# The running sum's row of a stick-breaking attention: two copies on two engines, or one on VectorE

## The reference, cut to what matters

```
z = q . k / 8                                   # scores of keys against queries
log_1m_beta = where(key < query, log_sigmoid(-z), 0)
between = reverse_cumsum(log_1m_beta) - log_1m_beta     # sum over the keys between
weights = where(key < query, exp(log_sigmoid(z) + between), 0)
out = weights @ v
```

## Time and profile before

| what | us |
|---|---|
| median of 3 runs | 1442.71 |
| lowest, highest | 1438.63, 1443.05 |
| the profiled execution | 1436.79 |
| its span, first to last instruction | 1435.1 |
| TensorE busy (modelled) | 1358.9 |
| VectorE busy | 871.1 |
| ScalarE busy | 676.8 |
| GpSimd busy | 324.5 |

### The profile page before, as it was taken

The page is one execution under the profiler, slowest core; times in us unless marked ns, Lnnn a source line. Parts: engine busy times, 40 slices in busy tenths (PEclk is TensorE's granted clock), DMA queues, the critical chain, the costliest instruction groups (busy, mean ns, idle before and its releaser), DMA issues. The chain is left out here.

```text
span 1435.1 us, 27696 instructions
## 1 busy us (share of the span) xinstructions
PE 1358.9 (95%) x11020; PEld 1063.8 (74%) x11020; DVE 871.1 (61%) x1347; ACT 676.8 (47%) x1249; POOL 324.5 (23%) x434
## 2 busy tenths in 40 slices
PE   6999989999999899898999889999999999999997
PEld 5877767777777566555677678888887788888886
DVE  6244261575752465667365787776665656669865
ACT  5533241352423387878354645445443434345541
POOL 6675544542432042435101300000000000000000
PEclk9999999999999799999999999999999999999999
DMA  6555333533225330404242254445444865787952
GB/s 204 145 156 150 103 82 89 149 85 84 62 75 125 122 75 3 90 2 137 89 156 103 81 165 159 142 147 158 157 136 147 279 194 179 257 269 252 305 188 103
DMA packets 191546, 201.07 MB, mean 140 GB/s; under 512 B 36669, under 2 KB 127994, under 8 KB 191418
## 3 DMA queue, kind: packets, MB, share of 16 engines
q1 hardware_dynamic: 145132, 169.47, 37.5%
q10 hardware_dynamic: 46286, 29.84, 7.5%
HBM read 145.06 MB, written 54.20 MB: 139 GB/s over the span
## 5 line engine op out<-in xcount | busy, mean ns | idle before, releaser
L484 POOL TENSOR_TENSOR fr_wL<-fr_raw,fr_wH 128x256 fp32r<-128x256 f32 (+1 forms) x208 | 164.2, 821 | 76.6 <-PE fr_ps_F L1267 54.2
L1267 PE MATMUL fr_ps_F<-fr_hL,fr_wH 128*128 128x512 f32 (+1 forms) x416 | 167.9, 404 | 2.8 <-DVE fr_hL L804 2.4
L1267 PE MATMUL fr_ps_F<-fr_hH,fr_wH 128*128 128x512 f32 (+1 forms) x416 | 166.6, 400 | 0.0
L1267 PE MATMUL fr_ps_F<-fr_hH,fr_wL 128*128 128x512 f32 (+1 forms) x416 | 113.4, 402 | 0.0
L1267 PEld LDWEIGHTS fr_ps_F<-fr_hL,fr_wH 128*128 128x128 f32 (+1 forms) x416 | 76.6, 184 | 22.9 <-issue 3.1
L2618 PE MATMUL all_ps_b<-ro_hH,ro_slot 128*128 128x512 f32 x272 | 88.4, 391 | 3.0 <-ACT pl_p L2120 1.5
L1267 PEld LDWEIGHTS fr_ps_F<-fr_hH,fr_wL 128*128 128x128 f32 (+1 forms) x416 | 76.2, 187 | 20.0 <-issue 3.2
L1267 PEld LDWEIGHTS fr_ps_F<-fr_hH,fr_wH 128*128 128x128 f32 (+1 forms) x416 | 76.8, 185 | 18.8 <-issue 2.3
L478 POOL CAST fr_wH<-fr_raw 128x1024 fp32r<-128x1024 f32 (+1 forms) x42 | 48.5, 1155 | 160.3 <-PE fr_ps_F L1267 140.0
L2627 PE MATMUL all_ps_b<-ro_hH 128*128 128x512 f32 x312 | 75.9, 389 | 0.0
L2627 PE MATMUL all_ps_b<-ro_y 128*128 128x512 f32 x300 | 72.7, 389 | 0.5 <-DVE ro_y L2454 0.5
(11 more groups left out here) (480 smaller groups left out, 3154.9 us busy)
## 6 DMA issues: line engine op xcount, KB each, us to landing
pl_slot<-in_w_ff SPq DMA_DIRECT2D x88, 256.0 KB, 4.4
pl_slot<-second_operands SPq DMA_DIRECT2D x75, 256.0 KB, 3.7
fr_raw<-in_w_in ACTq DMA_DIRECT2D x37, 512.0 KB, 4.2
second_operands<-pl_hL SPq DMA_DIRECT2D x64, 256.0 KB, 2.0
pl_hT<-in_w_ff SPq DMA_DIRECT2D x44, 256.0 KB, 4.5
projected<-fr_stage ACTq DMA_DIRECT2D x39, 256.0 KB, 4.4
pl_hT<-second_operands SPq DMA_DIRECT2D x37, 256.0 KB, 3.8
pl_xt<-in_w_ff SPq DMA_DIRECT2D x16, 512.0 KB, 5.6
```

Source lines behind the costliest of these rows:

```text
L484: m = pool.tensor_tensor(wL[b][:, k:k + 2, 0:wd], raw[b][:, k:k + 2, 0:wd], wH[b][:, k:k + 2, 0:wd].bitcast(F32), ALU.subtract)
L1267: m = pe.matmul(F[b][0:wd, :], w[b][:, k, 0:wd], a[:, k, :], start=(at_ == 0), stop=(at_ == len(passes) - 1))
```

## The change

The running sum's row is copied once, by VectorE, straight from the bank into row 0 of `SP[(u+2) % 4]`; ScalarE's copy, GpSimd's copy and the four `row` tiles are gone. VectorE makes it for unit u at the head of its turn u+3, before that turn's softplus, and for unit 25 (u = 27, NU - AHEAD) right behind the last softplus. The copy waits for unit u's weight. TensorE's wait before it reuses a bank is now on `placed`, with the same count.

```diff
-        row = [r.sb(f"row{n}", [1, HALF]) for n in range(4)]
@@ gpsimd
                     if not first:
-                        known = UNITS[u - 2][3]
-                        pool.wait_ge(s("handed"), handed(i, u - 2))
-                        pool.wait_ge(s("sp"), i * NU + u + 1)
-                        pool.tensor_copy(SP[u % 4][0:1, known:HALF], row[(u - 2) % 4][0:1, known:HALF]
-                                         ).then_inc(s("placed"), 1)
                         gla(i * NG + NTH[u] - 1)
@@ scalar
-                def hand_on(u):
-                    off = UNITS[u][3]
-                    if u >= 4 and hands_on(u - 4):
-                        act.wait_ge(s("placed"), placed(i, u - 2))
-                    act.copy(row[u % 4][0:1, off:HALF], Z[u % NZ][0:1, off:HALF]).then_inc(s("handed"), 1)
                 for u in range(NU):
                     weight(u)
-                    if hands_on(u):
-                        hand_on(u)
                     if u + AHEAD < NU:
@@ vector
+                def hand_on(u):
+                    off = UNITS[u][3]
+                    dve.wait_ge(s("weight"), i * NU + u + 1)
+                    dve.wait_ge(s("sp"), i * NU + u + 3)
+                    dve.tensor_copy(SP[(u + 2) % 4][0:1, off:HALF], Z[u % NZ][0:1, off:HALF]).then_inc(s("placed"), 1)
+
                 for u in range(NU):
+                    if u >= AHEAD and hands_on(u - AHEAD):
+                        hand_on(u - AHEAD)
                     softplus(u)
+                    if u == NU - 1:
+                        hand_on(NU - AHEAD)
@@ tensor, scores
                     if u >= NZ and hands_on(u - NZ):
-                        pe.wait_ge(s("handed"), handed(i, u - NZ))
+                        pe.wait_ge(s("placed"), handed(i, u - NZ))
```

## The result

The changed kernel takes 1503.66 us (median of 6 runs, 1496.99 to 1508.54). The kernel before, run on the same chip, takes 1441.42 us (6 runs, 1438.63 to 1443.43). The ratio is 1.0432, with a 95% interval from 1.0403 to 1.0460: 62 us slower, where 9 were predicted. The sign was right, the size was not, and the time lies far outside the range.

The account below looks back on a forecast made before the run. No engine plainly full in the heads stage: ScalarE paces part, an engine ring the rest. Order loses 15 us, ScalarE's relief wins 6: 9 us slower, 1451.7 us; range 1440 to 1463, the forecast's own 1447 to 1460.

Parts of the forecast that it names:

- What bounds it: Stage of the heads, 490 to 691 us: no engine plainly full; ScalarE sets the pace in part, an engine ring elsewhere.
- an ordered ring of engines: Over two turns: scores, exponential, logarithm, ratio part, other VectorE work, copy, next scores; 3.4 us plus other work when wide.
- ScalarE's relief, 6 us: 72 row copies leave ScalarE: 1 us won in late pass 2, 5 in narrow stretches; bounds 0 and 20.
- Load on VectorE: 72 copies from PSUM added, about 33 us or 27 by start spacing; VectorE, busy 128 of 201 us, still fits.
- The order term: Heads stage: the copy stands behind VectorE's other work, and TensorE's sums and scores wait; 15 us lost, bounds 2 and 25.
- I take 4 for about five such places: Narrow stretches: short copies, but a few turns have 2 to 4 us of other VectorE work; 4 us lost.
- the 5 us set by analogy for pass 1: Pass 1: same GLA pieces as pass 0, two units later, engines no fuller; 5 us lost, against 6 in pass 0.
- Rival (c): Passes 0 and 1, wide stretches: idling TensorE is granted a lower clock, 13 us on top, 22 us slower; chance 0.08.
- (a): Heads stage: ScalarE's relief is what counts, VectorE's idle time takes the copies; 7 us faster, 1435.7 us; chance 0.16.
- (b): Heads stage: bursts lose 6 to 8 us, ScalarE and the freed GpSimd port return it; 1442.7 us; chance 0.16.
- The marks to look for: Heads stage: copies 30 to 36 us, TensorE's waits 10 or more, pass 0 wide 5 longer, pass 2 wide no longer.

Follow-up runs that it names:

- e7: Changed kernel with every row copy cut to 4 columns, leaving out the running sum of the others: 1486.72 us, ratio 1.0337 to the kernel before.
- e13: Kernel before, both old copies kept, plus a VectorE read of each row at the head of turn u+3 that the scores wait for: 1512.55 us, ratio 1.0511.
- e5: Kernel before with ScalarE's and GpSimd's row copies cut to 4 columns, leaving out the running sum of the others: 1432.82 us, ratio 0.9958.
- e9: e2 with VectorE's placing of the row moved right behind the ratio part it waits for, ahead of the turn's other work: 1438.99 us, ratio 1.0013.
- e10: Changed kernel plus 37 TensorE matmuls of zeros, 256 columns each, in 16 turns where TensorE waited for the copy: 1492.68 us, ratio 1.0372.
- e2: Changed kernel, but ScalarE copies the row out of the bank again and VectorE only puts it in place, at turn u+3's head: 1448.87 us, ratio 1.0076.
- e4: Kernel before plus 69 VectorE additions of the row's width at the head of the turn, for which TensorE does not wait: 1459.54 us, ratio 1.0141.

## Why the prediction was right or wrong

**What bounds it: half right.** I called it "an ordered ring of engines" besides ScalarE, and let the ring's length count only where I walked through it. It was the main fact: with no engine full, an instruction put into the ring lengthens it (e7, e13).

**ScalarE's relief, 6 us: right in size in the kernel before.** e5 gives 6 us for ScalarE and GpSimd together; which of the two it comes from was not told apart. No run shows how much of it is left in the changed kernel.

**Load on VectorE, "it still fits on average": right about work beside the ring, wrong for work inside it.** The durations were right (0.67 us, 32.8 us in all). e9 carries 28.5 us of one-row copies for nothing that can be told. But in the ring 22 us of copy durations are worth 14 us (e7).

**The order term, 15 us with bounds of 2 and 25: this step failed, by its size.** The stage lost 66 us. The mechanism was named as it is: "new, the scores of unit u+4 (the bank is released by the same semaphore)", behind everything else of the turn. Where it was worked out it was right: 4.2 and 5.0 us were forecast between the three scores of pass 0, and 4.04 and 4.95 came. What failed is what I did not walk: "I take 4 for about five such places" in the narrow stretches, and the 5 us set by analogy for pass 1. The starts of the same unit's weight, after minus before, give what was lost where, with the lower clock and ScalarE's relief in it. Units 0 to 17 are those on the diagonal, nearly all narrow:

| units | later at their end, us | lost in them, us | order term predicted, us |
|---|---|---|---|
| pass 0, 0 to 17, up to the weight of 18 | 13.0 | 13.0 | share of 4 |
| pass 0, 18 to 27 | 24.6 | 11.6 | 6 |
| pass 1, 0 to 17 | 40.6 | 16.0 | share of 4 |
| pass 1, 18 to 27 | 52.5 | 11.9 | 5 |
| pass 2, 0 to 17 | 65.5 | 13.0 | share of 4 |
| pass 2, 18 to 26 | 66.0 | 0.5 | 0 |

The wide units lose 24 us where I had 11, part of it at the lower clock. The narrow ones lose 42 where I had 4: this is the size that was most wrong. (Cut at VectorE's ratio part of unit 18, as in the first table, it is 34 and 32; both are too small in the forecast by either cut.) The narrow loss comes in 15 steps of 1.0 to 5.4 us from one unit to the next, 38 of the 42 us, and not in five of 0.8. In pass 0, 8.9 us are lost by the weight of unit 17, at a clock of 0.82 against 0.84, so most of this is not the clock. I priced these units by their short copies, but the copy's length is the small part (e7): what counts is what stands in front of it. One such place in pass 0, from the changed kernel:

```profile
516.96 0.68 DVE L3407 COPY sb_O<-all_ps_b 128x512 f32<-128x512 f32 x1
...
517.56 0.68 DVE L3027 TENSOR_TENSOR gla_A<-all_ps_b,gla_eye 128x512 f32<-128x512 f32 x1
...
518.16 1.01 DVE L3032 TENSOR_TENSOR gla_qin<-gla_qin,gla_q 128x512 f32<-128x512 f32 x1
...
519.09 1.10 DVE L3036 TENSOR_TENSOR gla_kout<-gla_kout,gla_k 128x512 f32<-128x512 f32 x1
...
520.11 0.15 DVE L3434 COPY sb_E<-all_ps_b 1x8 f32<-1x8 f32 x1
...
520.40 0.56 PE L3518 MATMUL all_ps_b<-early_qL,early_kS 128*128 128x262 f32 x1 [2.82 <-DVE sb_E L3434]
```

A copy of 8 columns, 0.15 us long, stands behind four pieces of other work, and the scores wait 2.82 us for it. In a ring the fill of an engine ("VectorE's work fills it no more") says little; what counts is the other work of each single turn, and whom it waits for. Pass 2's wide part has only one short piece per turn and came nearly as forecast: a period of 2.15 us (weights at 741.43 and, four later, at 750.04) against the 2.10 of the earlier trace rows, where I had expected a little less than before; VectorE is busy 22.8 of its 25.4 us.

**Rival (c), the clock, given 0.08: its mechanism came in.** I priced it at 13 us, as something that could be added to the forecast. It is there (104 us at the lower level against 25), and e10 shows at least about 9 us of it. The runs don't separate the whole of its price; TensorE is shown busy 29.6 us longer for the same work. It was also too unlikely in my list: the waits which the forecast itself predicted are those in which TensorE idles.

**Rivals (a) and (b): wrong.** What decides against (a) is as I wrote: at the place that was 540 to 546 us before and is 555 to 565 us now, TensorE waits for the copy (1.22, 2.48 and 1.00 us).

**The marks to look for.** VectorE's copies, the waits before the first scores matmul and the longer wide part of pass 0 came as named. The wide part of pass 2, "no longer than now", is 1.6 us longer. "10 us or more in total" was 48.3.

In sum, by the runs: freeing the bank by VectorE's copy at the head of turn u+3 costs some 51 us net of ScalarE's relief (changed against e2), with the tie to the ratio part, the other work in front, the copy's duration and the lower clock included; placing the row late costs 9 us (e2 against e9); the remaining 0.1% can't be told from nothing.

## What to carry to other kernels

An instruction that frees a buffer belongs on an engine and at a place in its queue where nothing slow stands in front of it; before two jobs are merged into one instruction, ask who waited for each, and give the merged one the place that the more urgent needs. When no engine is full, don't sum loads: walk through the ring for every turn, since one walked place that comes out right says nothing about those taken as even. And where a change adds waits of TensorE as here (19 of 1.0 to 4.1 us in one stage), count the lower clock in as part of the forecast, not as a separate accident.

## What the runs showed of the hardware

- More work made a kernel faster. 37 added matmuls of zeros in the waits raised the stage's granted clock from 0.81 to 0.92 and shortened the run by about 9 us (e10), though nothing uses the added products. In the changed kernel two sums matmuls of the same shape took 1.12 us at clock 1.00 and 2.07 us at 0.50.
- A one-row copy from PSUM on VectorE costs by its columns and not by its partitions: 0.67 us for 1x512, where the 128x512 copy took 0.69 us, and 0.147 us for 1x4 (e7).
- A VectorE addition with two SBUF inputs over one row took 1.05 us in the mean at 512 wide beside GpSimd's copies (e4), and GpSimd's own copies went up from 581 to 747 ns. In the kernel before the same VectorE subtraction took 686 ns in the median and 2155 at the most, and the cut of keys that took 2.08 us beside a copy of GpSimd's took 1.32 us in the changed kernel, without one. That one engine holds up the other is argued from this, not shown by a run of its own.
